# Attention on one Trainium2 core: scores and query projections placed between value products, and probabilities scaled on GpSimd instead of ScalarE

## The reference, cut to what matters

```python
# branch A (MLA), per head: queries by low-rank projection, nope and rope parts
s = (qn @ kn.T + qr @ kr.T) * scale
o_a = softmax(s) @ v
# branch B (GQA), 8 query heads over 2 key/value heads
s = qb @ kb.T * scale
o_b = softmax(s) @ vb
```

## Time and profile before

| | us |
|---|---|
| three runs | 2192.65, 2194.33, 2194.97; median 2194.33 |
| profiled execution, first to last instruction | 2192.3 |
| TensorE busy | 2110.8 (96%) |
| VectorE busy | 875.9 (40%) |
| ScalarE busy | 564.0 (26%) |
| GpSimd busy | 4.7 (0%) |

### The profile page before, as it was taken

How to read it: one execution, slowest core, us unless ns; L and a number is a source line. 1 busy time by engine, 2 the same in 40 slices (tenths; PEclk the granted TensorE clock), 3 DMA queues, 4 the chain that set the end, 5 groups by cost and what they waited for, 6 DMA issues and landing times.

```text
span 2192.3 us, 26368 instructions
## 1 busy us (share of the span) xinstructions
PE 2110.8 (96%) x10319; PEld 1373.3 (63%) x10319; DVE 875.9 (40%) x1246; ACT 564.0 (26%) x998; POOL 4.7 (0%) x8
## 2 busy tenths in 40 slices
PE   7999999999999999999999899998999989998986
PEld 5787888888887777888888545353534444444432
DVE  4762667666676665346333301112020302021114
ACT  4263432222246664113222511010101110011102
POOL 0000000000000000000000000000000000000000
PEclk9999999999999999999999999999999999999999
DMA  9948675887760001533422799999999999999998
GB/s 364 385 162 297 231 259 200 318 305 280 281 231 25 25 1 57 178 131 128 164 87 87 309 392 408 426 426 428 427 427 427 428 428 427 427 428 427 426 422 308
DMA packets 144063, 634.81 MB, mean 290 GB/s; under 512 B 11986, under 2 KB 29544, under 8 KB 112756
## 3 DMA queue, kind: packets, MB, share of 16 engines
q1 hardware_dynamic: 139348, 625.38, 72.5%
q10 hardware_dynamic: 4640, 8.40, 1.0%
HBM read 621.15 MB, written 12.58 MB: 289 GB/s over the span
## 4 chain that ended last, share of the span: by engine, by line
PE 84%; DMA 12%; DVE 2%; ACT 1%; issue 0%; SPq 0%; DVEq 0%; ACTq 0%
PE bank L804 24%; PE bank L1311 23%; PE bank L806 13%; DMA e_wide<-in_w_e_up 10%; PE bank L1283 5%; PE bank L990 5%; PE bank L864 3%; PE bank L1083 3%; PE bank L1303 1%; PE bank L1071 1%; DMA e_slot<-in_w_e_down 1%; PE bank L1304 1%; PE bank L769 1%; PE bank L1293 1%; PE bank L1195 1%
## 5 line engine op out<-in xcount | busy, mean ns | idle before, releaser
L1311 PE MATMUL bank<-e_wide,xgT 128*64 128x512 f32 x1456 | 404.5, 606 | 42.7 <-DMA e_wide<-in_w_e_up 26.4
L1492 ACT ACTIVATE w_hi<-stage 128x1024 fp32r<-128x1024 f32 (+1 forms) x168 | 175.4, 1044 | 594.5 <-PE bank L804 339.8
L1918 DVE TENSOR_TENSOR w_lo<-stage,w_hi 128x1024 fp32r<-128x1024 f32 (+1 forms) x168 | 202.4, 1205 | 302.6 <-ACT w_hi L1492 302.0
L1311 PEld LDWEIGHTS bank<-e_wide,xgT 128*64 128x64 f32 x1456 | 130.8, 139 | 285.1 <-issue 284.2
L1311 PE MATMUL bank<-e_slot,xgT 128*64 128x512 f32 x584 | 207.0, 598 | 0.0
L1311 PE MATMUL bank<-e_wide,heT 128*64 128x512 f32 x672 | 167.4, 594 | 0.0
L804 PE MATMUL bank<-hT_hi,w_hi 128*128 128x512 f32 x512 | 159.1, 392 | 0.0
L804 PE MATMUL bank<-hT_lo,w_hi 128*128 128x512 f32 x512 | 157.9, 390 | 0.0
L804 PE MATMUL bank<-hT_hi,w_lo 128*128 128x512 f32 x512 | 157.7, 389 | 0.0
L2490 DVE TENSOR_TENSOR x<-x,bank 128x512 f32<-128x512 f32 x128 | 79.6, 682 | 191.8 <-PE bank L1304 190.3
L1993 DVE SCALAR_TENSOR_TENSOR ada_acc<-ada_tile,siluc,ada_acc 128x1024 f32<-128x1024 f32 x116 | 148.8, 1282 | 6.7 <-DMA ada_tile<-in_w_ada 1.0
(11 more groups left out here) (363 smaller groups left out, 2961.4 us busy)
## 6 DMA issues: line engine op xcount, KB each, us to landing
e_wide<-in_w_e_up SPq DMA_DIRECT2D x49, 2048.0 KB, 17.3
e_wide<-in_w_e_gate SPq DMA_DIRECT2D x42, 2048.0 KB, 15.1
e_wide<-in_w_e_down SPq DMA_DIRECT2D x42, 2048.0 KB, 17.2
ada_tile<-in_w_ada SPq DMA_DIRECT2D x156, 512.0 KB, 5.8
stage<-in_w_in SPq DMA_DIRECT2D x96, 512.0 KB, 6.6
e_slot<-in_w_e_gate SPq DMA_DIRECT2D x43, 1024.0 KB, 16.4
e_slot<-in_w_e_down SPq DMA_DIRECT2D x41, 1024.0 KB, 17.1
e_slot<-in_w_e_up SPq DMA_DIRECT2D x30, 1024.0 KB, 10.8
```

Of the source, the lines that this page charges most:

```text
L1311: last = mm(acc[h][64 * e:64 * e + 64, :], stationary(e), weights(h, e), start=first, stop=end)
L1492: A(w_hi[:, c % NSPLIT, :, 0:width], stage[:, c % NSTAGE, :, 0:width], ACT.Copy).then_inc(hi_ready, 1)
L1918: V.tensor_tensor(w_lo[:, c % NSPLIT, :, 0:width], stage[:, c % NSTAGE, :, 0:width], w_hi[:, c % NSPLIT, :, 0:width].bitcast(F32), ALU.sub ...
```

## The change

TensorE: in `attend_rest` of a GQA head, score block 0 of the next GQA head is put between probs_t 3 and times_v 2, block 1 between times_v 2 and times_v 3; blocks 2 and 3 stand where pairs stood before. In `attend_rest` of an MLA head, the first projection of the next turn (uqr if that turn is even, uq if it is odd) is put between times_v 2 and times_v 3. ScalarE no longer multiplies the probabilities; GpSimd does. The sums are inverted in two halves, and the orders of VectorE and ScalarE are changed to match.

```diff
 TensorE
+            def queries(i):
+                pe.wait_ge(hw_lo, split_of(i, "uq"))
+                split_product(query_bank(i), ..., True, True).then_inc(proj_done, 1)
+
+            def project_first(i):
                 pe.wait_ge(pro_ready, QUERY[i] + 1)
                 if i % 2 == 0:
                     pe.wait_ge(hw_lo, split_of(i, "uqr"))
                     split_product(bank[5][:, :], ...)
+                else:
+                    queries(i)
+
+            def project(i):
+                if i % 2 == 0:
                     if i:
                         pe.wait_ge(o_lo, 2 * i)
-                pe.wait_ge(hw_lo, split_of(i, "uq"))
-                split_product(query_bank(i), ...)
+                    queries(i)
                 pe.wait_ge(hw_lo, split_of(i, "uk"))
...
                 probs_t(a, 3)
+                if a % 2 == 0 and a < 2 * HM - 2:
+                    gqa_scores(a // 2 + 1, (0,))
                 times_v(a, 2)
+                if a < 2 * HM - 2:
+                    if a % 2:
+                        project_first(a // 2 + 1)
+                    else:
+                        gqa_scores(a // 2 + 1, (1,))
                 times_v(a, 3)
...
             gqa_scores(0, range(4))
+            project_first(0)
...
-                    gqa_scores(i + 1, (0, 1))
+                    gqa_scores(i + 1, (2,))
                     probs_t(2 * i + 1, 0)
                     probs_t(2 * i + 1, 1)
-                    gqa_scores(i + 1, (2, 3))
+                    gqa_scores(i + 1, (3,))
                     attend_rest(2 * i + 1)
 ScalarE
-            def normalise(a):
...
-                exponentials(2 * i + 1, 12, range(3))
+                exponentials(2 * i + 1, 12, (0, 1))
                 if i < HM - 1:
                     item_hi(QUERY[i + 1])
                 else:
                     hi(N_BR + 1, 1)
+                exponentials(2 * i + 1, 12, (2,))
                 exponentials(2 * i + 1, 12, (3,))
-                normalise(2 * i + 1)
                 output_hi(2 * i)
                 if i < HM - 1:
-                    exponentials(2 * i + 2, i + 1, range(4))
-                    normalise(2 * i + 2)
+                    exponentials(2 * i + 2, i + 1, (0,))
...
 VectorE
+            def inverse_sums(a, half):
                 b = a % 2
+                dve.wait_ge(exp_done, 4 * a + 2 * half + 2)
+                V.reciprocal(rsum[:, b, 4 + 2 * half:6 + 2 * half], rsum[:, b, 2 * half:2 * half + 2]).then_inc(rinv_seq, 1)
...
                 negative_max(2 * i + 1, 12, range(4))
-                probs_transposed(2 * i, 2)
+                inverse_sums(2 * i + 1, 0)
                 if i < HM - 1:
                     item_lo(QUERY[i + 1])
-                inverse_sums(2 * i + 1)
+                probs_transposed(2 * i, 2)
+                inverse_sums(2 * i + 1, 1)
                 probs_transposed(2 * i, 3)
...
                 probs_transposed(2 * i + 1, 1)
-                    negative_max(2 * i + 2, i + 1, (2, 3))
+                    negative_max(2 * i + 2, i + 1, (2,))
                 probs_transposed(2 * i + 1, 2)
-                    inverse_sums(2 * i + 2)
+                    negative_max(2 * i + 2, i + 1, (3,))
                 probs_transposed(2 * i + 1, 3)
+                    inverse_sums(2 * i + 2, 0)
+                    inverse_sums(2 * i + 2, 1)
 GpSimd
+            def normalise(a):
+                b = a % 2
+                for qb in range(4):
+                    if qb % 2 == 0:
+                        pool.wait_ge(rinv_seq, 2 * a + qb // 2 + 1)
+                    last = G.tensor_scalar(probs[b][:, qb, :], probs[b][:, qb, :], rsum[:, b, 4 + qb:5 + qb], None, ALU.mult)
+                last.then_inc(p_ready, 1)
+
+            for a in range(HM + HG):
+                normalise(a)
```

More of the change, by code:

```diff
@@ L1000, in query_bank @@
                 return bank[4 + i % 2][:, :]
-            def project(i):
+            def queries(i):
+                pe.wait_ge(hw_lo, split_of(i, "uq"))
+                split_product(query_bank(i), by_k(4, lambda k: three(uq_hi[:, k, :], uq_lo[:, k, :], cqT_hi[:, k, :], cqT_lo[:, k, :])),
+                              True, True).then_inc(proj_done, 1)
+            def project_first(i):
                 pe.wait_ge(pro_ready, QUERY[i] + 1)
@@ L1008, in project @@
                                   True, True).then_inc(proj_done, 1)
+                else:
+                    queries(i)
+            def project(i):
+                if i % 2 == 0:
                     if i:
                         pe.wait_ge(o_lo, 2 * i)
-                pe.wait_ge(hw_lo, split_of(i, "uq"))
-                split_product(query_bank(i), by_k(4, lambda k: three(uq_hi[:, k, :], uq_lo[:, k, :], cqT_hi[:, k, :], cqT_lo[:, k, :])),
-                              True, True).then_inc(proj_done, 1)
+                    queries(i)
                 pe.wait_ge(hw_lo, split_of(i, "uk"))
@@ L1707, in head_inputs @@
                 A(qn_hi[:, :], bank[4 + i % 2][:, :], ACT.Copy).then_inc(proj_hi, 1)
-                if i == 0:
-                    normalise(0)
                 act.wait_ge(proj_done, projected(i) + pair + 2)
@@ L1733, in _ @@
                         head_uqr_hi(i + 1)
-                else:
+                if i == HM - 1:
                     act.wait_ge(s_done, 4 * (2 * i + 1) + 1)
@@ L1744, in _ @@
                     hi(N_BR + 1, 1)
+                exponentials(2 * i + 1, 12, (2,))
                 exponentials(2 * i + 1, 12, (3,))
-                normalise(2 * i + 1)
                 output_hi(2 * i)
                 if i < HM - 1:
-                    exponentials(2 * i + 2, i + 1, range(4))
-                    normalise(2 * i + 2)
-            hi(N_BR + 2, 2)
+                    exponentials(2 * i + 2, i + 1, (0,))
+                if i < HM - 1:
+                    exponentials(2 * i + 2, i + 1, (1,))
+                else:
+                    hi(N_BR + 2, 2)
+                if i < HM - 1:
+                    exponentials(2 * i + 2, i + 1, (2,))
+                if i < HM - 1:
+                    exponentials(2 * i + 2, i + 1, (3,))
             output_hi(2 * HM - 1)
@@ L2230, in output_lo @@
                 V.tensor_tensor(oT_lo[:, k, :], bank[4][:, :], oT_hi[:, k, :].bitcast(F32), ALU.subtract).then_inc(o_lo, 1)
-            def inverse_sums(a):
+            def inverse_sums(a, half):
                 b = a % 2
-                dve.wait_ge(exp_done, 4 * a + 4)
-                V.reciprocal(rsum[:, b, 4:8], rsum[:, b, 0:4]).then_inc(rinv_seq, 1)
+                dve.wait_ge(exp_done, 4 * a + 2 * half + 2)
+                V.reciprocal(rsum[:, b, 4 + 2 * half:6 + 2 * half], rsum[:, b, 2 * half:2 * half + 2]).then_inc(rinv_seq, 1)
             def probs_transposed(a, kt):
@@ L2255, in head_rests @@
                     if i == 0:
-                        inverse_sums(0)
+                        inverse_sums(0, 0)
+                        inverse_sums(0, 1)
                     dve.wait_ge(proj_hi, n + 1)
```

## The result

The changed kernel takes 2203.35 us, the median of 5 runs (2202.15 to 2204.84), against 2194.33 (2192.65 to 2196.02): ratio 1.0042, with a 95% interval of 1.0029 to 1.0055. It is slower by 9.0 us. Forecast were 2198.0 us, a range of 2192.5 to 2202.5, and 0.37 for "slower"; the time lies above the range.

A forecast was written before the change was run, and what follows sets the result against it. TensorE was taken as the bound, busy 2110.8 of 2192.3 us. Gaps -1.9, even turns +4.9, turn 3 +0.5 and format switches +0.2 gave +3.7 onto the median: 2198.0 us, range 2192.5 to 2202.5.

The forecast's parts named there:

- What there is to win: 8.1 us: TensorE's gaps in the attention: 7.8 us in turns 0 to 6 plus 0.3 in turn 3, 0.37% in all.
- The GQA head: covers cost nothing, 0.19 won: GQA head's times_v 2 and 3: inserted score blocks of 0.69 us cover the copies, gaining 0.19 us.
- GpSimd's multiplications: Scaling of probabilities moved from ScalarE: at 1.15 us apiece hidden, cost 0; nothing lost up to 1.43 apiece.
- the nearest row: GpSimd's product of two inputs, 1.149 us in the profile, taken as the price (1.15) of each moved multiplication.
- times_v 0 waits 0.84 for its copy: MLA head's times_v 0: chain of 2.99 us against a cover of 2.24, waiting 0.84 us in place of 0.39.
- Even turns, +4.9: Before uq in turns 2, 4 and 6: TensorE waits 1.6 us each for bank 4's hand-over, +4.9 us.
- Turn 3, +0.5: Key transposition into bank 5 waits for qn_lo: 0.83 us instead of 0.3, +0.5 us.
- ScalarE relieved: 0: ScalarE's 41 us of multiplications were off TensorE's path but for placing output_hi, so removing them gains 0.
- Rival 1: GpSimd late at p_ready of every MLA head, from 1.43 us apiece; at 1.75, +9 us, 2207; chance 0.12.
- Rival 2: Bank 4's hand-over before uq is covered after all: turns 2, 4, 6 pay nothing, 2193.1 us; chance 0.12.
- rival 3: Covers work throughout the attention without new waits: all 8.1 us come back, 2186.2 us; chance 0.08.
- rival 4: Inserted TensorE blocks wait for something and run where they did: 2194.3 to 2195 us; chance 0.03.

The follow-up runs named there:

- e6: Changed kernel with all multiplications on ScalarE and VectorE's maximum 1 of the next GQA head moved ahead of output_lo: 2192.29 us, ratio 0.9990 to the kernel before.
- e1: Changed kernel with the multiplications back on ScalarE, by halves of the inverted sums, all other orders as changed: 2197.08 us, ratio 1.0014 to the kernel before.
- e3: Changed kernel with GpSimd's tensor_scalar replaced by a two-input tensor_tensor product of the same values: 2198.28 us, ratio 1.0014 to the kernel before.
- e4: Changed kernel with uqr's 12 passes split, 4 before times_v 3 and 8 behind it: 2198.15 us, ratio 1.0014 to the kernel before.
- e5: Changed kernel with GpSimd multiplying blocks 0 and 1 and ScalarE blocks 2 and 3: 2197.44 us, ratio 1.0019 to the kernel before.
- e7: e6 with uqr's 12 passes also split, 4 before and 8 behind times_v 3: 2188.47 us, ratio 0.9976 to the kernel before.
- e8: e7 with GpSimd multiplying blocks 0 and 1 and ScalarE blocks 2 and 3: 2187.71 us, ratio 0.9970 to the kernel before.
- e9: Kernel before with only the multiplications moved to GpSimd, in the two-input form: 2198.45 us, ratio 1.0026 to the kernel before.

## Why the prediction was wrong, point by point

- *What there is to win: 8.1 us.* It held: the best version took 7.3 of them (a stretch of 211.73 against 204.45), and turn 3's, which the change makes larger, is still there.
- *The GQA head: covers cost nothing, 0.19 won.* Right, by the starts.
- *GpSimd's multiplications: 0, "up to 1.24 us apiece; nothing up to 1.43".* This is the step that failed, a mis-sized term: 1.15 was taken and 1.56 measured (6.18 us for four). The rest of the step fits. GpSimd does start at 682.1 (683.92 less the 1.8 of the turn) and TensorE does ask at 687.1; by its own formula 682.1 + 6.2 is 1.2 us too late, and in the trace GpSimd ends at 690.10 where TensorE was ready at 688.89. e6, whose turns have neither this wait nor the one at times_v 0, gives the loss over all seven turns: 1.34 us each in the changed kernel, 0.85 in e1. That is 3.5 us in seven turns.
- *The first head.* The prediction wrote no term for it. It loses 1.1 us (its transpositions start 16.41 us into the stretch, and 15.29 in e1). The price of 1.56 alone would just have been in time; what made it late are the 1.1 us that two of its products took longer, beside VectorE's work. The prediction had weighed this very thing, but for uqr_lo, where it does cost nothing. No run takes VectorE's work away, so that this is its cause rests on the overlap in the trace. 3.5 and 1.1 are the 4.6 us by which the stretches of the changed kernel and e1 differ, of the 5.4 between forecast and result; the rest is 0.1 in e1's stretch against the sum (3.8 for 3.7) and 0.6 outside the stretch. e3, which changes the form of that one instruction, gives the forecast time.
- *The choice of the nearest row* was the fault in method: same engine, but another form, taken as the price although nothing in the trace made it an upper bound. It was also a mean over four with one long one among them. The upper end was open, and the range should have carried it.
- *The rule weighed beside it.* The Trainium skill (GPSIMD Engine Reference, Engine selection) has one-input work at roughly line rate and two-input work slower. Here it is the other way round, 1.56 against 1.04 us on 128 x 512; the measurement decides.
- *times_v 0 waits 0.84 for its copy.* Right where it can be seen: it is hidden behind GpSimd's wait in the changed kernel; e1 has 7 waits of 0.6 from the modelled end, and e6 takes them away with 5.9 us, 0.85 each.
- *Even turns, +4.9.* Right: 1.7 us each against 1.6, and e4 gives 4.9 back.
- *Turn 3, +0.5.* The wait is there (0.6 for qn_lo); it was not tested alone. From turn 2's query transposition to turn 3's key transposition e1 takes 0.33 us more than the kernel before (710.17 to 728.66 against 710.14 to 728.30), where -0.27 + 0.53 = 0.26 was forecast.
- *ScalarE relieved: 0.* Right for this kernel (e5 against e1), wrong for the better ones (e7 against e8).
- *Rival 1* was what happened, in its mechanism and place; its price line at 1.56 us is 1.2 late, 0.5 beyond the wait that is there, 3.5 us in seven turns, and with the first head gives 2202.6 us. A chance of 0.12 was too low for an operation without a row. Rival 2 falls by the waits before uq, rival 3 by those at times_v 0 in e1, rival 4 by the starts: the inserted blocks run where they were put.

## What to carry to other kernels

Price a moved operation by its own form on the new engine, and where no row shows it, leave the upper end open; here the break-even of 1.43 us was passed by 0.13. Read a price from the shortest and the median, not from a mean over a few rows in which another engine may have been in the way. When work is put between a producer and the wait that it used to cover, ask what stands behind the producer now: uqr had been hiding a 1.6 us hand-over, and four of its twelve passes were enough in the new place, with eight left behind to cover it (no other split was tried). In fixed queues look for operations that are ready early and stand behind a late one: moving one maximum ahead of a waiting subtraction was worth 5.9 us.

## What the runs showed of the hardware

- GpSimd on 128 x 512 fp32, undisturbed: a product with one tensor and a factor per row 1.56 us, four in 6.18; with a constant four in 6.14; with two tensors 1.04, four in 4.03, in e3 with one number per row repeated as the second, and 1.04 for the earlier trace rows, where both inputs are repeated patterns.
- TensorE's granted clock: 1.00 after idle times of 1.2 to 1.5 us; 0.52 in the first 2.5 us after one of 3.25 us and 0.75 in the next 2, in a stretch otherwise busy, at a price of 1.5 us.
- GpSimd's product of two tensors and a VectorE subtraction with two SBUF inputs wait for each other where they overlap: 0.45 us on each side in e9, 0.89 for VectorE and 0.45 for GpSimd in turn 1 of e3, 0 and 0.54 where both start together. With the one-input form VectorE's uqr_lo loses 0.11 and GpSimd nothing, but beside VectorE's qr_lo and uq_lo, which start ahead, two GpSimd products take 1.98 and 2.23 instead of 1.56.
